# Attention weights: four of ten key tiles turned by DMA in 16-bit halves instead of by TensorE, with the value product placed later

## Chip, cores and metric

The kernel runs on one core of one Trainium2 chip. The metric is the device time of one execution in microseconds (us), lower is better. Engines are TensorE (PE in the rows; PEld its weight loads), VectorE (DVE), ScalarE (ACT), GpSimd (POOL) and SyncE (SP), which here only issues DMAs.

## What is computed

One step of a hybrid backbone over 1024 latent tokens and 128 prompt tokens: a modulated norm, an input projection, a gated MLP, a pooling mixer and latent attention side by side, an output projection, then 16 expert-choice routed experts. The change is in the attention alone. All is float32.

```python
def attention(q, k, v):
    ...
    def block(qi):
        s = jnp.einsum('bqhd,bkhd->bhqk', qi, k).astype(jnp.float32) * ATTN_SCALE
        pr = jax.nn.softmax(s, axis=-1).astype(v.dtype)
        return jnp.einsum('bhqk,bkhd->bqhd', pr, v)
```

There are 8 heads with 64 value columns each. A latent query sees 1280 keys (1024 latent, 256 cached); a prompt query sees the 128 prompt keys.

## The kernel before

The attention runs from about 274 to 650 us. It works on head pairs: four groups i = 0 to 3 of two heads. A group has 18 score tiles n = 0 to 17; tile n is token tile t = n // 2 and head j = n % 2. Tiles 0 to 15 are 128 latent queries by 1280 keys (ten key tiles of 128), tiles 16 and 17 are the prompt's, 128 by 128.

For one tile n the steps are:

- `score` (line 881, TensorE): 128 queries by 512, 512 and 256 keys into three PSUM banks. Two sets of three banks alternate, so score n waits for the exponential of n-2.
- `highest` (lines 1863 and 1865, VectorE): the row maximum over 1280 columns, and its negation.
- `exponential` (line 1455, ScalarE): exp into the SBUF tile `prob[n % 2]`, with row sums.
- `scaled` (lines 1884 and 1886, VectorE): reciprocal of the sum, and the weights times it, in place. It raises `norm_ok`.
- `turn` (line 915, TensorE): ten 128x128 transposes in three chunks (4, 4 and 2 key tiles) into PSUM banks 6 and 7.
- `turned` (line 1443 ScalarE, line 1897 VectorE): each chunk copied to `probT`. VectorE takes the first chunk of odd tiles, ScalarE all others.
- `weigh` (line 930, TensorE): for two tiles at once (both heads of a token tile), ten key tiles of values times `probT`, in one PSUM bank; `weighed` (line 1877, VectorE) copies it out.

Every engine runs its instructions in the order in which they are written. `attend` of each engine is a loop over n = 2, 4, ..., 14 and a written-out last part. TensorE's last part also takes `fill(0)` to `fill(5)`: the next group's query and key projections, or in the last group four half tiles of the output projection. `MID_ORDER` lists who takes banks 6 and 7 in turn. After a group, `scores_values` makes the next group's values and first two score tiles.

SyncE's queue loads in the attention the next group's weights (`head_queries`, `head_keys`) and moves the rope rows of the next group's queries (`move_queries`, line 535). In the last group it loads the 4 MB of output weights and, before the attention, two tiles of the input rows (`x_again`). GpSimd has nothing to do from before the attention to its last part, where it adds `x_again` to the output rows (line 2461).

The expert stage, later, already turns two arrays by DMA in 16-bit halves: 128 rows of 1024 float32 are split into high and low 16-bit halves by VectorE, turned by `dma_start_transpose` (512 KB; lines 606 and 615) and joined by VectorE (lines 2273 and 2281).

## Time and profile before

| | |
|---|---|
| median of 3 runs | 1561.43 us (1561.3 to 1561.96) |
| the profiled execution | 1561.85 us |
| its span | 1560.0 us |
| TensorE granted clock, mean | 0.996 |
| TensorE, VectorE, ScalarE, GpSimd busy | 98%, 39%, 27%, 7% |
| attention, four groups | about 274 to 650 us |
| experts | from 781 us on |

The span runs from the first to the last instruction of the profiled execution. Busy time is the time in which an engine has at least one instruction in it. Matmuls are pipelined: a matmul's record is longer than its distance to the next, so the pace of TensorE is read from the distance of starts.

### The profile page before, as it was taken

The numbers are of one execution on the slowest core, as the hardware profiler recorded it, in microseconds if no ns is written. First come the engines' busy times: TensorE is split into PE (matmuls) and PEld (weight loads), VectorE is DVE, ScalarE is ACT, GpSimd is POOL, SyncE is SP. The second block draws the span as 40 slices with busy tenths as digits, with TensorE's granted clock in tenths as the row PEclk, the third lists the DMA queues.
The fourth block names the chain that finished last, engine by engine and source line by source line (L and its number), as shares of the span: only waits on it lengthen the run. The fifth ranks groups of instructions, "written<-read, shape, count | busy, mean of one in ns | idle before, by whom it ended". The sixth has DMA issues, their size and how long they took to land.

```text
span 1560.0 us, 25914 instructions
## 1 busy us (share of the span) xinstructions
PE 1529.3 (98%) x10585; PEld 1224.9 (79%) x10585; DVE 607.6 (39%) x1389; ACT 423.0 (27%) x965; POOL 106.8 (7%) x108
## 2 busy tenths in 40 slices
PE   6999999999999999999999999999999999999997
PEld 3654545666666676544599999999999999999996
DVE  2211546675657576125666222222222222222215
ACT  2400112555545454223522111111111111111114
POOL 0005300000000000111000001000000000000000
PEclk9999999999999999999999999999999999999998
DMA  9970002001010300262278899999899899899885
GB/s 366 349 251 35 31 2 65 8 1 27 0 27 0 120 9 1 69 215 95 102 282 307 284 297 360 304 302 297 316 301 360 297 299 303 308 309 354 282 267 223
DMA packets 178634, 305.21 MB, mean 196 GB/s; under 512 B 73811, under 2 KB 75386, under 8 KB 176398
## 3 DMA queue, kind: packets, MB, share of 16 engines
q1 hardware_dynamic: 173534, 286.01, 52.5%
q0 software_dynamic: 4752, 17.30, 4.3%
q8 instruction: 43, 0.70, 0.2%
q10 hardware_dynamic: 288, 1.05, 0.2%
q14 instruction: 17, 0.14, 0.0%
HBM read 266.18 MB, written 21.64 MB: 184 GB/s over the span
## 4 chain that ended last, share of the span: by engine, by line
PE 93%; DVE 3%; DMA 1%; ACT 1%; issue 1%; SPq 0%; DVEq 0%; ACTq 0%; POOLq 0%
PE ps L1252 31%; PE ps L1281 16%; PE ps L881 9%; PE ps L644 8%; PE ps L982 7%; PE ps L930 5%; PE ps L915 4%; PE ps L669 2%; PE ps L835 2%; PE ps L659 1%; PE ps L847 1%; PE ps L860 1%; PE ps L676 1%; DMA wreg<-x_rows 1%; PE ps L736 1%
## 5 line engine op out<-in xcount | busy, mean ns | idle before, releaser
L1252 PE MATMUL ps<-mreg,wreg 128*128 128x144 f32 x4096 | 506.3, 286 | 0.0
L1252 PEld LDWEIGHTS ps<-mreg,wreg 128*128 128x128 f32 x4096 | 503.4, 190 | 0.7 <-ACT hreg L1567 0.4
L1281 PE MATMUL ps<-mreg,wreg 128*128 128x144 f32 x2048 | 257.4, 287 | 1.9 <-DVE mreg L2299 1.9
L1281 PEld LDWEIGHTS ps<-mreg,wreg 128*128 128x128 f32 x2048 | 254.1, 191 | 2.3 <-DVE mreg L2299 2.2
L2299 DVE TENSOR_TENSOR mreg<-ps,mreg 128x144 f32<-128x144 f32 x128 | 39.4, 308 | 357.5 <-PE ps L1252 346.7
L881 PE MATMUL ps<-wreg 128*128 128x512 f32 (+2 forms) x400 | 171.7, 519 | 0.2
L1604 ACT ACTIVATE mreg<-ps 128x144 f32<-128x144 f32 x128 | 37.2, 291 | 426.1 <-PE ps L1252 426.1
L982 PE MATMUL ps<-wreg,mreg 128*128 128x512 f32 x288 | 130.8, 598 | 0.0
L644 PE MATMUL ps<-hreg,wreg 128*128 128x512 f32 (+1 forms) x400 | 128.9, 480 | 0.0
L915 PEld LDWEIGHTS ps<-const,hreg 128*128 128x128 f32 x648 | 79.8, 140 | 58.8 <-issue 39.3
L1863 DVE TENSOR_REDUCE stat<-ps 128x1 f32<-128x1280 f32 (+1 forms) x72 | 97.7, 1357 | 57.4 <-PE ps L881 57.3
L644 PEld LDWEIGHTS ps<-hreg,wreg 128*128 128x128 f32 x400 | 64.6, 191 | 62.2 <-issue 61.9
L1443 ACT ACTIVATE hreg<-ps 128x512 f32<-128x512 f32 (+2 forms) x172 | 82.1, 502 | 101.9 <-PE ps L915 100.2
L1455 ACT ACTIVATE hreg<-ps,stat 128x1280 f32<-128x1280 f32 (+1 forms) x72 | 88.1, 1223 | 69.0 <-DVE stat L1865 69.0
L1623 ACT ACTIVATE mreg<-ps,modT 128x128 f32<-128x128 f32 x128 | 47.0, 367 | 210.7 <-PE ps L1281 210.7
L2244 DVE COPY hreg<-mreg 128x256 uint16<-128x256 uint16 x112 | 33.1, 295 | 178.9 <-ACT hreg L1625 178.9
L915 PE MATMUL ps<-const,hreg 128*128 128x128 f32 x648 | 97.5, 274 | 0.0
L982 PEld LDWEIGHTS ps<-wreg,mreg 128*128 128x128 f32 x288 | 52.0, 190 | 54.1 <-issue 54.1
L930 PEld LDWEIGHTS ps<-hreg,wreg 128*64 128x64 f32 x1296 | 70.0, 137 | 22.6 <-ACT hreg L1443 15.3
L930 PE MATMUL ps<-hreg,wreg 128*64 128x128 f32 x1296 | 78.5, 275 | 0.9 <-ACT hreg L1443 0.9
L881 PEld LDWEIGHTS ps<-wreg 128*128 128x128 f32 x400 | 62.1, 190 | 15.5 <-issue 13.6
L1886 DVE TENSOR_SCALAR hreg<-hreg,stat 128x1280 f32<-128x1280 f32 (+1 forms) x72 | 60.1, 835 | 2.6
(305 smaller groups left out, 1123.1 us busy)
## 6 DMA issues: line engine op xcount, KB each, us to landing
wreg<-in_w_e_dram SPq DMA_DIRECT2D x96, 2048.0 KB, 11.9
wreg<-in_w_ada_dram SPq DMA_DIRECT2D x16, 1024.0 KB, 8.5
wreg<-in_w_ada_dram SPq DMA_DIRECT2D x16, 512.0 KB, 11.0
wreg<-in_x_sample_dram SPq DMA_DIRECT2D x8, 512.0 KB, 4.6
wreg<-in_w_out_dram SPq DMA_DIRECT2D x1, 4096.0 KB, 12.9
x_rows<-wreg SPq DMA_DIRECT2D x8, 512.0 KB, 2.8
xn_rows<-wreg SPq DMA_DIRECT2D x8, 512.0 KB, 2.8
wreg<-x_rows SPq DMA_DIRECT2D x8, 512.0 KB, 8.8
```

The lines of the kernel that those rows point to most:

```text
L644: mm = pe.matmul(bank[BANK[n]][:, 0:gn], w_in_sb[:, k, w_at + m * P:w_at + (m + 1) * P], hT[:, k, g0:g0 + gn], start=(k == 0), stop=(k == ...
L881: mm = pe.matmul(bank[3 * (n % 2) + ch][:, 0:kn], qT[:, j, t * P:(t + 1) * P], kT[:, j, k0:k0 + kn], start=True, stop=True)
L915: mm = pe.transpose(bank[MID_BANK[("turn", n, ch)]][:, a * P:(a + 1) * P], prob[n % 2][:, kt * P:(kt + 1) * P], ident)
L930: mm = pe.matmul(pv_at(t)[64 * j:64 * j + 64, :], v_sb[:, kt, 64 * j:64 * j + 64], probT[:, 2 * (t % 2) + j, src * P:(src + 1) * P], start ...
L982: mm = pe.matmul(bank[o_bank(x)], mixT[:, k, t * P:(t + 1) * P], w_out_sb[:, k, hf * 512:(hf + 1) * 512], start=(k == 0), stop=(k == KD - 1))
L1252: mm = pe.matmul(o[:, 0:CAP], w[s][:, k, (f % 4) * P:(f % 4 + 1) * P], xsT[b][:, k, :], start=(k == 0), stop=(k == KD - 1))
L1281: mm = pe.matmul(bank[4 + dm % 2][:, 0:CAP], w2[f // 4][:, f % 4, dm * P:(dm + 1) * P], hidT[:, f, :], start=(f == 0), stop=(f == 7))
L1443: act.activation(probT[:, 2 * (t % 2) + j, ch * 512:ch * 512 + w], bank[MID_BANK[("turn", n, ch)]][:, 0:w], ACT.Copy).then_inc(t_out, 1)
L1455: act.activation(prob[n % 2][:, 0:w], src, ACT.Exp, bias=a_neg[:, n % 4:n % 4 + 1], scale=SCALE, accum_out=a_sum[:, n % 4:n % 4 + 1]).then ...
L1623: act.activation(yT[:, dm, :], bank[4 + dm % 2][:, 0:CAPS], ACT.Copy, scale=modT[:, 0, 40 + dm:41 + dm])
L1863: dve.tensor_reduce(a_max[:, r:r + 1], src, AX_X, ALU.max).then_inc(max_ok, 1)
L1886: dve.tensor_scalar(prob[n % 2][:, 0:w], prob[n % 2][:, 0:w], a_rec[:, r:r + 1], None, ALU.mult).then_inc(norm_ok, 1)
```

## The change

For score tiles 0 to 15 the first chunk (key tiles 0 to 3, 512 of 1280 columns) is no longer turned by TensorE. Instead:

- GpSimd (`split_prob`) copies the 512 float32 columns of `prob[n % 2]`, read as 1024 16-bit numbers, to `prob_halves[n % 2]`: first all low halves, then all high halves. It waits for `norm_ok` of n and for the transpose of n-2.
- SyncE (`turn_prob`) issues one DMA transpose of these 128 rows by 1024 halves (256 KB) to `prob_halves_T[n % 4]`.
- `joined(n)` writes the halves back in pairs to `probT`: ScalarE for even n, VectorE for odd n.
- `exponential(n)` also waits for the split of n-2, which reads the buffer that it overwrites.
- `weigh` takes key tiles 4 to 9 first, then 0 to 3 behind a wait for both joins. In the loop it stands behind all three score chunks of tile n instead of the first.
- The orders of the loops on TensorE, VectorE and ScalarE change. The maximum and the exponential of tile n-1 move to the iteration of n.
- In SyncE's queue the 16 transposes of a group stand ahead of `move_queries`. In the last group the output weights come in eight pieces, one behind each of the first eight transposes, and `x_again` is loaded behind the last joins.
- Waits on `t_mm` count 34 turns in a group instead of 50; the expert stage's waits on the shared semaphores start from the attention's count.

The core of the diff:

```diff
+        prob_halves = [view(wreg, 23232 + s * 512, 512).bitcast(U16) for s in range(2)]
+        prob_halves_T = [view(wreg, 16384 + s * 512, 512).bitcast(U16).rearrange("p (c q) -> p c q", q=P) for s in range(4)]
...
+        def join_prob(eng, copy, i, n):
+
+            t, j = divmod(n, 2)
+            eng.wait_ge((x_turned, y_turned)[j], (i * 8 + t + 1) * 16)
+            return copy(probT[:, 2 * (t % 2) + j, 0:512].bitcast(U16).rearrange("p (c h) -> p h c", h=2),
+                        prob_halves_T[n % 4].rearrange("p (h k) q -> p h (k q)", h=2))
...
-            for t in range(2):
-                sp.dma_start(x_again[t], tok_rows(x_sample, x_prompt, t)).then_inc(xa_in[t], 16)
...
-            for i in range(1, 4):
-                sp.wait_ge(wq_ok, i)
-                head_queries(i)
-                sp.wait_ge(proj_mm, i * 9)
-                head_keys(i)
-                sp.wait_ge(s_mm, i * 18)
-                move_queries(i)
+            def turn_prob(i, n):
+                sp.wait_ge(halves_split, prob_split(i, n))
+                sp.dma_start_transpose(out=prob_halves_T[n % 4], in_=prob_halves[n % 2]).then_inc((x_turned, y_turned)[n % 2], 16)
+            for i in range(3):
+                sp.wait_ge(wq_ok, i + 1)
+                head_queries(i + 1)
+                turn_prob(i, 0)
+                sp.wait_ge(proj_mm, (i + 1) * 9)
+                head_keys(i + 1)
+                for n in range(1, 16):
+                    turn_prob(i, n)
+                sp.wait_ge(s_mm, (i + 1) * 18)
+                move_queries(i + 1)
             sp.wait_ge(q_moved, 4 * 64)
-            sp.dma_start(w_out_sb, w_out[0].rearrange("(k p) f -> p k f", p=P)).then_inc(w_out_in, 16)
-            sp.wait_ge(proj_mm, 36)
-            sp.dma_start(flip_sb, flip_count).then_inc(flip_in, 16)
+            for n in range(16):
+                turn_prob(3, n)
+                if n < KD:
+                    sp.dma_start(w_out_sb[:, n, :], w_out[0, n * P:(n + 1) * P, :]).then_inc(w_out_in, 16)
+                if n == 1:
+                    sp.wait_ge(proj_mm, 36)
+                    sp.dma_start(flip_sb, flip_count).then_inc(flip_in, 16)
+            for t in range(2):
+                turn_out(sp, 3, 12 + 2 * t, 0)
+                turn_out(sp, 3, 13 + 2 * t, 0)
+                sp.dma_start(x_again[t], tok_rows(x_sample, x_prompt, t)).then_inc(xa_in[t], 16)
...
                 def weigh(t):
 
-                    if t < 7:
-                        turn_out(pe, i, 2 * t + 1, 0)
                     turn_out(pe, i, 2 * t + 1, 1 if t < NT - 1 else 0)
                     bank_free(("weigh", t))
-                    for kt in range(10) if t < NT - 1 else range(10, 11):
+                    for kt in (4, 5, 6, 7, 8, 9, 0, 1, 2, 3) if t < NT - 1 else (10,):
                         if kt == 8:
                             turn_out(pe, i, 2 * t + 1, 2)
+                        if kt == 0:
+
+                            turn_out(pe, i, 2 * t, 0)
+                            turn_out(pe, i, 2 * t + 1, 0)
                         for j in range(2):
                             src = kt if t < NT - 1 else 0
                             mm = pe.matmul(pv_at(t)[64 * j:64 * j + 64, :], v_sb[:, kt, 64 * j:64 * j + 64],
                                            probT[:, 2 * (t % 2) + j, src * P:(src + 1) * P],
-                                           start=(kt in (0, 10)), stop=(kt in (9, 10)))
+                                           start=(kt in (4, 10)), stop=(kt in (3, 10)))
                     mm.then_inc(pv_mm, 1)
 
                 for n in range(2, 16, 2):
                     score(i, n, 0)
+                    turn(n - 2, 1)
+                    score(i, n, 1)
+                    turn(n - 2, 2)
+                    score(i, n, 2)
                     if n >= 4:
                         weigh((n - 4) // 2)
-                    score(i, n, 1)
-                    turn(n - 2, 0)
-                    score(i, n, 2)
-                    turn(n - 2, 1)
-                    turn(n - 2, 2)
-                    for ch in range(3):
-                        score(i, n + 1, ch)
-                        turn(n - 1, ch)
+                    score(i, n + 1, 0)
+                    turn(n - 1, 1)
+                    score(i, n + 1, 1)
+                    turn(n - 1, 2)
+                    score(i, n + 1, 2)
...
+                def joined(n):
+
+                    join_prob(act, lambda out, src: act.activation(out, src, ACT.Copy), i, n).then_inc(t_out, 1)
+
                 def exponential(n):
 
                     act.wait_ge(neg_ok, i * 18 + n + 1)
                     if n >= 2:
 
-                        act.wait_ge(t_mm, i * 50 + 3 * (n - 1))
+                        if n < 16:
+                            act.wait_ge(t_mm, i * 34 + 2 * (n - 1))
+                        act.wait_ge(halves_split, prob_split(i, n - 2))
...
+                for n in range(2, 16, 2):
+                    if n >= 4:
+                        joined(n - 4)
+                    turned(n - 2, 1)
+                    if n >= 4:
+                        exponential(n - 1)
+                    turned(n - 2, 2)
                     exponential(n)
-                    if n >= 2:
-                        turned(n - 1, 1)
-                        turned(n - 1, 2)
-                    exponential(n + 1)
-                    turned(n, 0)
-                    if n < 16:
-                        turned(n, 1)
+                    turned(n - 1, 1)
+                    turned(n - 1, 2)
...
+                def joined(n):
+
+                    join_prob(dve, dve.tensor_copy, i, n).then_inc(t_out_d, 1)
+
                 scaled(0)
                 highest(i, 1)
                 values_out(i, 2)
                 scaled(1)
-                def turned(n):
-
-                    t, j = divmod(n, 2)
-                    dve.wait_ge(t_mm, i * 50 + turns_before(n, 0) + 1)
-                    dve.tensor_copy(probT[:, 2 * (t % 2) + j, 0:512], bank[MID_BANK[("turn", n, 0)]]).then_inc(t_out_d, 1)
-
                 for n in range(2, 16, 2):
+                    if n >= 4:
+                        highest(i, n - 1)
+                        joined(n - 3)
                     highest(i, n)
-                    turned(n - 1)
-                    highest(i, n + 1)
+                    if n >= 4:
+                        scaled(n - 1)
+                        weighed((n - 4) // 2)
                     scaled(n)
-                    weighed((n - 2) // 2)
-                    scaled(n + 1)
...
+            def split_prob(i, n):
+
+                pool.wait_ge(norm_ok, i * 18 + n + 1)
+                if n >= 2:
+                    pool.wait_ge((x_turned, y_turned)[n % 2], (i * 8 + n // 2) * 16)
+                pool.tensor_copy(prob_halves[n % 2].rearrange("p (h k) -> p h k", h=2),
+                                 prob[n % 2][:, 0:512].bitcast(U16).rearrange("p (k h) -> p h k", h=2)).then_inc(halves_split, 1)
+            for i in range(4):
+                for n in range(16):
+                    split_prob(i, n)
...
+DVE_JOINS = [(n, 0) for n in range(1, 16, 2)]
```

TensorE's loop, some iterations in. Line 881 (905 after) is score, 915 (939) turn, 930 (956) weigh; the rows without a tile are waits; `hreg` holds `prob` and `probT`, `wreg` the queries, keys and values. TensorE's loop before, from the wait ahead of an iteration's first score:

```order
L876 REGISTER_ALU
L881 MATMUL ps<-wreg 128x512
L428 REGISTER_ALU
L930 MATMUL ps<-hreg,wreg 64x128 x16
L428 REGISTER_ALU
L930 MATMUL ps<-hreg,wreg 64x128 x4
L881 MATMUL ps<-wreg 128x512
L915 MATMUL ps<-const,hreg 128x128 x4
L881 MATMUL ps<-wreg 128x256
L906 REGISTER_ALU
L915 MATMUL ps<-const,hreg 128x128 x4
L428 REGISTER_ALU
```

TensorE's loop after, from the last score chunk of tile n-1 to the first part of the value product:

```order
L905 MATMUL ps<-wreg 128x256
L900 REGISTER_ALU
L905 MATMUL ps<-wreg 128x512
L434 REGISTER_ALU
L939 MATMUL ps<-const,hreg 128x128 x4
L905 MATMUL ps<-wreg 128x512
L434 REGISTER_ALU
L939 MATMUL ps<-const,hreg 128x128 x2
L905 MATMUL ps<-wreg 128x256
L434 REGISTER_ALU
L956 MATMUL ps<-hreg,wreg 64x128 x12
L434 REGISTER_ALU
```

Before, an iteration starts with one score chunk, the value product, a chunk of scores, and then turns in three chunks of a tile. Now all three score chunks of a tile have the turns of chunks 1 and 2 between them, and the value product follows the third; its second part waits for the joins.

VectorE's loop. Line 1863 (1903 after) is the maximum, 1865 (1905) its negation, 1884 and 1886 (1924 and 1926) reciprocal and scaling, 1897 the eviction of a turned chunk, 1877 (1917) the copy of a value product, 440 the join (`wreg` holds `prob_halves_T`). VectorE's loop before, from the first maximum of an iteration:

```order
L1863 TENSOR_REDUCE stat<-ps 128x1 [waits s_mm]
L1865 TENSOR_SCALAR stat<-stat 128x1 [waits max_ok]
L1896 REGISTER_ALU
L1897 COPY hreg<-ps 128x512 [waits t_mm]
L1862 REGISTER_ALU
L1863 TENSOR_REDUCE stat<-ps 128x1 [waits s_mm]
L1865 TENSOR_SCALAR stat<-stat 128x1 [waits max_ok]
L1884 RECIPROCAL stat<-stat 128x1 [waits exp_ok]
L1886 TENSOR_SCALAR hreg<-hreg,stat 128x1280 [waits rec_ok]
L1876 REGISTER_ALU
L1877 ISA [waits pv_mm]
L1877 COPY mreg<-ps 128x128
```

VectorE's loop after, from the first maximum of an iteration:

```order
L1903 TENSOR_REDUCE stat<-ps 128x1 [waits s_mm]
L1905 TENSOR_SCALAR stat<-stat 128x1 [waits max_ok]
L439 ISA
L440 COPY hreg<-wreg 128x2x512 [waits y_turned]
L1902 REGISTER_ALU
L1903 TENSOR_REDUCE stat<-ps 128x1 [waits s_mm]
L1905 TENSOR_SCALAR stat<-stat 128x1 [waits max_ok]
L1924 RECIPROCAL stat<-stat 128x1 [waits exp_ok]
L1926 TENSOR_SCALAR hreg<-hreg,stat 128x1280 [waits rec_ok]
L1916 REGISTER_ALU
L1917 ISA [waits pv_mm]
L1917 COPY mreg<-ps 128x128
```

Before, VectorE evicts a chunk that TensorE turned between the two maxima. Now at this place it joins a chunk that a DMA turned, and the second maximum and the scaling behind it stand behind that DMA.

## Rows read from the trace of the kernel before

**Rows 1.** Page, part 1, and busy time of one whole group of the attention loop.

```profile
PE 1529.3 (98%) x10585; PEld 1224.9 (79%) x10585; DVE 607.6 (39%) x1389; ACT 423.0 (27%) x965; POOL 106.8 (7%) x108
364.00:454.00 90.00, 89.82 (x663) 61.91 (x662) 56.70 (x100) 48.93 (x88) 0.00 (x0) 1.00 0.05 12
```

**Rows 2.** Timeline, TensorE: start us, duration us, line, operation; one round.

```profile
389.28 2.40 PE L930 MATMUL ps<-hreg,wreg 128*64 128x128 f32 x40
...
391.61 1.12 PE L881 MATMUL ps<-wreg 128*128 128x512 f32 x2
...
395.00 0.60 PE L915 MATMUL ps<-const,hreg 128*128 128x128 f32 x4
...
395.43 1.02 PE L881 MATMUL ps<-wreg 128*128 128x512 f32 x2
...
398.34 2.40 PE L930 MATMUL ps<-hreg,wreg 128*64 128x128 f32 x40
```

**Rows 3.** Page, part 5: all 648 transposes; count, busy us, mean ns.

```profile
L915 PE MATMUL ps<-const,hreg 128*128 128x128 f32 x648 | 97.5, 274 | 0.0
```

**Rows 4.** Timeline, VectorE, of the same pair.

```profile
393.64 1.49 DVE L1863 TENSOR_REDUCE stat<-ps 128x1 f32<-128x1280 f32 x1 [0.32 <-PE ps L881]
...
395.63 0.69 DVE L1897 COPY hreg<-ps 128x512 f32<-128x512 f32 x1 [0.31 <-PE ps L915]
...
397.37 1.49 DVE L1863 TENSOR_REDUCE stat<-ps 128x1 f32<-128x1280 f32 x1 [1.04 <-PE ps L881]
...
398.96 0.15 DVE L1884 RECIPROCAL stat<-stat 128x1 f32<-128x1 f32 x1
...
399.15 0.89 DVE L1886 TENSOR_SCALAR hreg<-hreg,stat 128x1280 f32<-128x1280 f32 x1
```

**Rows 5.** Groups by line: 16-bit joins of the expert stage, and one ScalarE pass.

```profile
L2273 DVE COPY hreg<-hreg 128x2048 uint16<-128x2048 uint16 x14 | 18.4, 1318 | 0.0
L1502 ACT ACTIVATE wreg<-wreg 128x1024 f32<-128x1024 f32 x7 | 7.4, 1057 | 24.9 <-POOL wreg L2461 24.9
```

**Rows 6.** GpSimd's groups: instruction, count, busy us, mean ns.

```profile
L2461 POOL TENSOR_TENSOR wreg<-wreg 128x1024 f32<-128x1024 f32 x7 | 16.5, 2353 | 480.4 <-DVE wreg L1950 480.4
L2481 POOL COPY mreg<-hreg 128x128 f32<-128x128 f32 x16 | 12.7, 797 | 10.5 <-ACT hreg L1567 10.5
L2441 POOL MEMSET wreg<- 128x1184 f32 x2 | 2.2, 1084 | 14.9 <-DVE wreg L1769 14.9
```

**Rows 7.** Timeline: VectorE's scaling beside a GpSimd instruction, and without one.

```profile
630.68 0.69 DVE L1950 TENSOR_TENSOR wreg<-ps,g_rows 128x512 f32<-128x512 f32 x1 [6.39 <-PE ps L982]
...
631.45 2.35 POOL L2461 TENSOR_TENSOR wreg<-wreg 128x1024 f32<-128x1024 f32 x1 [390.34 <-DVE wreg L1950]
...
632.51 1.38 DVE L1886 TENSOR_SCALAR hreg<-hreg,stat 128x128 f32<-128x128 f32 x1
...
640.09 0.29 DVE L1886 TENSOR_SCALAR hreg<-hreg,stat 128x128 f32<-128x128 f32 x1
```

**Rows 8.** DMA issues: KB each, us from issue to landing.

```profile
wreg<-wreg SPq DMA_DIRECT2D x16, 144.0 KB, 2.5
hreg<-hreg SPq DMA_TRANSPOSE x14, 4.3
mreg<-mreg SPq DMA_TRANSPOSE x13, 16.2
```

**Rows 9.** One transpose of 512 KB: its issue on SyncE, then the DMA engines.

```profile
931.38 1.98 SPq L606 DMA_TRANSPOSE hreg<-hreg  x1
...
932.00:932.50 0.50, 0.50 (x6) 0.50 (x6) 0.00 (x0) 0.01 (x1) 0.00 (x0) 1.00 0.00 0
932.50:935.00 2.50, 2.50 (x22) 2.50 (x22) 0.64 (x2) 0.28 (x1) 0.00 (x0) 1.00 1.09 204
```

**Rows 10.** Timeline: the rope rows' move, and the next group's first scores.

```profile
440.24 2.42 SPq L535 DMA_DIRECT2D wreg<-wreg  x4
...
452.98 2.31 PE L881 MATMUL ps<-wreg 128*128 128x512 f32 x6
```

More of the change, by code:

```diff
@@ L382, in build, with prob_split @@
         x_turned, y_turned = sem("x_turned"), sem("y_turned")
+        def prob_split(i, n):
+            return i * 16 + n + 1
         def y_steps(e):
@@ L908, in turn @@
                 def turn(n, ch):
-                    if ch == 0:
+                    if ch < 2:
                         pe.wait_ge(norm_ok, i * 18 + n + 1)
@@ L2537, in turns_before @@
 def turns_before(n, ch):
[L2539 to L2547 removed]
+    return 2 * n + ch - 1 if n < 16 else 16 + n
+PROB_TURNS = 4 * 16
+DVE_JOINS = [(n, 0) for n in range(1, 16, 2)]
+ACT_TURNS = [u for n in range(2, 16, 2) for u in [(n - 4, 0)][:n // 4] + [(n - 2, 1), (n - 2, 2), (n - 1, 1), (n - 1, 2)]]
+ACT_TURNS += [(12, 0), (14, 0), (14, 1), (14, 2), (15, 1), (15, 2), (16, 0), (17, 0)]
+MID_ORDER = [u for n in range(2, 16, 2)
+             for u in [("turn", n - 2, 1), ("turn", n - 2, 2)] + [("weigh", (n - 4) // 2)][:n // 4]
+             + [("turn", n - 1, 1), ("turn", n - 1, 2)]]
+MID_ORDER += [("weigh", 6)] + [("turn", n, ch) for n in (14, 15) for ch in (1, 2)]
 MID_ORDER += [("turn", 16, 0), ("turn", 17, 0), ("weigh", 7), ("weigh", 8)]
```

62 lines of the change are left out of this document (33 added, 29 removed).

## The prediction

> **What bounds the kernel now.** I read the busy shares first, then one whole group of the attention loop, then one round of its inner loop in the timeline. TensorE has a matmul in flight for 98% of the span and for 89.8 of 90 us in the group at 364 to 454 us, at the full granted clock; VectorE works 56.7 us there, ScalarE 48.9 us, GpSimd not at all, and the DMA engines are 5% busy [rows 1]. A busy TensorE need not be at its peak, so I check the pace. One round (two 128-query score tiles of the same tokens, n and n+1) takes 398.34 - 389.28 = 9.06 us [rows 2]. In it four transposes go through in 395.43 - 395.00 = 0.43 us, 0.107 us each, with the next score right behind them; 0.107 and not the 274 ns of the record [rows 3] is what a transpose costs a full TensorE, since the record contains the pipeline. Twenty transposes are 2.14 us of the round, a value product (weigh) is near 2.3 us with its switch, and the rest is scores. So the attention loop is bound by TensorE's stream, and a transpose taken out is worth its 0.107 us, provided that nothing else comes to set the round.
>
> **What the change removes.** Four of ten transposes for each n below 16: 8 x 0.107 = 0.86 us of a round, which leaves 9.06 - 0.86 = 8.20 us. A group has 7 rounds in the loop (n = 2 to 14) and 8 more transposes in its last part. There are 4 groups. If TensorE stays the bound, the gain is 4 x (7 x 0.86 + 0.86) = 27.5 us. The five evictions of the first chunk's turned keys go as well: on VectorE 0.69 us [rows 4], on ScalarE one more.
>
> **What it adds, engine by engine.** For each n a GpSimd copy that splits 512 float32 weights into 1,024 16-bit halves, a DMA transpose of 256 KB on SyncE's queue, and a copy that joins the halves again, on VectorE for odd n and on ScalarE for even n.
>
> The join on VectorE: the same kind of copy over 2,048 halves takes 1.318 us [rows 5]. With about 0.15 us that doesn't depend on the size (my estimate, from the smallest VectorE instructions [rows 4]) half the size is 0.15 + 0.58 = 0.73 us, against 0.69 us for the eviction that it replaces. ScalarE's join, over 1,024 elements from SBUF, is taken as 1.06 us [rows 5]. ScalarE then works about 5.8 us of a round and VectorE about 6.4 us: by their sums neither is a bound.
>
> The split: no row shows it. Above it stands the GpSimd instruction that reads two streams of 1,024 elements and writes one, 2.35 us; below it the memset that only writes, 1.084 us for 1,184 elements, so 0.94 us for 1,024 [rows 6]. It reads one stream and writes one, so I take a value between, 1.5 us, and keep both ends. GpSimd then works some 3 us of a round. Farther off stands the copy of 128 elements in short pieces, 0.797 us, which is 6.2 ns an element [rows 6]; that is a rival below. The Trainium skill (GPSIMD Engine Reference, section on elementwise work) gives about 1.8 cycles an element for a tight loop, 512 elements in 769 ns; by it the split would be an estimated 1.54 us, and the sum would move by 0.04 us a round. The same page advises against GpSimd for elementwise work; here that matters only as far as the rounds below show.
>
> The DMA transpose: no row shows 256 KB. The expert stage has 512 KB: 4.3 us from issue to landing [rows 8]. Its data starts some 1.1 us after the issue, and runs at 204 GB/s for 2.5 us [rows 9], so 0.7 us come behind it. Half the data is 1.1 + 1.25 + 0.7 = 3.1 us. The bounds: 2.5 us, which a plain move of 144 KB takes, and 4.3 us [rows 8]. The other transpose's 16.2 us [rows 8] is time behind 4 MB of weights in the same queue; in the attention loop the DMA engines are nearly idle [rows 1], except in the last group, where eight 512 KB pieces of the output weights go between the transposes. I cost these at nothing: they come about once in 4 us and are read first in the tail. The Trainium skill (Advanced Engine Details and Errata, section on the X-bar transpose) expects 350 to 400 GB/s from a transpose. The trace differs, 204 GB/s, and the trace decides; by the page the transfer would be an estimated 0.6 us shorter, and TensorE would stay the bound.
>
> **The waits that it adds: the DMA round.** VectorE's new order in iteration n is: maximum n-1, join n-3, maximum n, scaling n-1, value out, scaling n. Behind join n-3 stand maximum n and scaling n-1, and scaling n-1 is what the split, the transpose and the join n-1 of the next iteration start from. So there is a closed round, once for two tiles: join 0.73; maximum, its negation, reciprocal and scaling in a row, 399.15 + 0.89 - 397.37 = 2.67 us [rows 4]; split 1.5; transfer 3.1; and five handoffs, of which the trace shows one (VectorE to GpSimd, 631.45 - 631.37 = 0.08 us [rows 7]), together some 0.3 us as an estimate. Sum: 0.73 + 2.67 + 0.3 + 1.5 + 3.1 = **8.3 us**. That is 0.1 us above TensorE's 8.20 us, and 0.76 us below 9.06. The round beats the old one as long as split plus transfer stay below 9.06 - 3.70 = 5.36 us; I have 4.6.
>
> The even tiles' joins on ScalarE come one iteration after the scaling plus a whole round, so they have some 4 us more, and the value product, which now takes keys 4 to 9 first and keys 0 to 3 last, has its joins ready. An exponential n now also waits for split n-2, since it overwrites the weights; that split ends over 3 us ahead of it.
>
> **The waits that it adds: the shared port.** A scaling of 128 elements takes 0.29 us alone, but 1.38 us where it starts while GpSimd's addition runs, and it ends at 633.89, right behind the addition's end at 633.80 [rows 7]. So a scaling that comes while a split runs waits for the split's end. The Trainium skill states the same (SBUF — State Buffer, Who interferes with whom: an exclusive lock for whole instructions); the trace agrees, with 1.38 against 0.29 us. Scaling n comes some 0.5 us behind scaling n-1, so split n-1 is in its way each time. This makes a second round: join, maximum, scaling n-1 (0.73 + 2.67), split n-1, scaling n (0.89), split n, and the join again if it also has to wait: 4.29 + 2 x (split + 0.17) = 7.6 us at a split of 1.5 us. It is below 8.2, so it costs nothing; at a split of 2.35 us it is 9.33 us, and it passes 9.06 at 2.2 us. The small weight scalings (0.3 us) come ahead of the split's handoff and cost nothing.
>
> **What is moved.** SyncE's queue now holds the transposes ahead of the rope rows' move for the next group. Before, that move is issued at 440.24 and the group's first score starts at 452.98 [rows 10]: 12.7 us for an issue of 2.4 us and a landing of 2.5 us [rows 8, 10]. It can come some 4 us later, behind transpose 15, and stays hidden. The value product of tile 7 and the prompt's stand behind the last fills, which gives joins 14 and 15 over 5 us. The reload of the input rows now stands behind these joins in the last group; each has two output products of 7 us of time. All these are put at nothing.
>
> **The sum.** 28 rounds x 0.76 = 21.3 us, and 32 transposes outside of them x 0.107 = 3.4 us: 24.7 us. The profiled execution took 1561.85 us and its span is 1560.0; the runs' median is 1561.43, 0.4 us lower. 1561.4 - 24.7 = **1537 us** (rounded).
>
> **Rivals.**
> 1. TensorE stays the bound (split plus transfer under 4.5 us): 27.5 us less, 1534. It differs from the forecast by 3 us and is counted with it. If the new order also loses switches of TensorE (0.5 us of a round is not stream), up to 4 us more: 1530.
> 2. The DMA round in between: split plus transfer at 4.9 to 5.2 us, round 8.6 to 8.9: 28 x 0.16 to 0.46 + 3.4 = 8 to 16 us less, 1545 to 1553. For it: both terms are interpolated, and both could be short by 0.3 us.
> 3. **Slower: the split is as slow as the two-stream addition.** At 2.35 us the port round is 9.33 us and the DMA round 3.70 + 2.35 + 3.1 = 9.15. TensorE then waits in every round: 28 x 0.27 - 3.4 = 4 us more, 1566. With the full transpose's 4.3 us as well, 10.35 us: 28 x 1.29 - 3.4 = 33 us more, 1594. It decides from a split of 2.2 us, or a sum of 5.36 us. For it: the nearest GpSimd row of the same length is just this one. Against it: half the reads.
> 4. The split costs by the element what the piecewise copy costs, 6.2 ns: 6.4 us, the port round 4.63 + 12.8 = 17.4 us, 28 x 8.4 = 235 us more, about 1793. Against it: that copy has 8 pieces of 16 elements, the split 2 of 512.
> 5. The gain isn't there because transposes weren't what TensorE was short of, within 3 us of 1561. The pace in rows 2 speaks against it.
>
> **Chances.** Forecast with rival 1: 0.55. Rival 2: 0.15. Rival 3: 0.22. Rival 4: 0.03. Rival 5: 0.05. For eight in ten I leave out rival 4, the far part of rival 3 and little below: 1530 to 1570. 0.2% is 3 us, about what a measurement of this kernel can tell from no change: faster 0.70, same 0.06, slower 0.24.
>
> **What would show it.** The round in the steady part of a group: 8.2 to 8.3 us, and TensorE's idle below 0.2 us a round. The split's mean near 1.5 us, the transpose's landing near 3.1 us. VectorE's join waiting for a DMA by a few tenths; that wait well over 1 us means rival 2 or 3. Scaling's mean rising from 0.89 us by some 0.4 us, half of them blocked. The forecast is wrong if split plus transfer exceed 5.36 us, if a join runs at half the rate that I took, or if the granted clock leaves 1.0 in the group because TensorE waits.

## The result, and the profile after

| | before | after |
|---|---|---|
| median | 1561.7 us (1561.3 to 1562.34, 4 runs) | 1535.84 us (1535.2 to 1536.37, 4 runs) |
| ratio | | 0.9835, 95% interval 0.9823 to 0.9848 |
| span of the profiled execution | 1560.0 us | 1533.9 us |

The changed kernel is 25.9 us faster; 1537 was forecast. The page's part 1 and the busy time of the same stretch of the attention loop, which answer to [rows 1]:

```profile
PE 1499.8 (98%) x10329; PEld 1196.6 (78%) x10329; DVE 614.5 (40%) x1393; ACT 439.1 (29%) x961; POOL 173.8 (11%) x172
364.00:454.00 90.00, 89.42 (x631) 59.38 (x630) 63.44 (x110) 54.64 (x89) 18.10 (x18) 1.00 0.32 63
```

TensorE runs 256 transposes fewer (4 key tiles x 16 x 4 groups) and is as full as before; VectorE, ScalarE and GpSimd work more; in this stretch the DMA engines go from 5% to 32% busy. TensorE's timeline shows the round, from one value product to the next (start, duration, line):

```profile
385.31 2.40 PE L956 MATMUL ps<-hreg,wreg 128*64 128x128 f32 x40
393.46 2.40 PE L956 MATMUL ps<-hreg,wreg 128*64 128x128 f32 x40
```

The round is 393.46 - 385.31 = 8.15 us, for 9.06 in [rows 2]. The added work, in rows of three views: GpSimd's split and the two joins (groups by line: count, busy us, mean ns, idle before), and the transposes (DMA issues of the second group: us from issue to landing).

```profile
L2507 POOL COPY wreg<-hreg 128x1024 uint16<-128x1024 uint16 x64 | 66.4, 1038 | 291.4 <-DVE hreg L1926 288.2 <-DMA wreg<-wreg 3.2
L440 DVE COPY hreg<-wreg 128x1024 uint16<-128x1024 uint16 x32 | 23.9, 748 | 2.0 <-DMA wreg<-wreg 1.9
L1473 ACT ACTIVATE hreg<-wreg 128x1024 uint16<-128x1024 uint16 x32 | 43.2, 1350 | 0.0
wreg<-wreg SPq DMA_TRANSPOSE x16, 3.1
```

VectorE's join waited for a transpose only twice in 32 times, 1.9 us in all. Its timeline, which answers to [rows 4], says what it waits for instead (idle before in brackets):

```profile
384.25 0.75 DVE L440 COPY hreg<-wreg 128x1024 uint16<-128x1024 uint16 x1
385.42 1.49 DVE L1903 TENSOR_REDUCE stat<-ps 128x1 f32<-128x1280 f32 x1 [0.42 <-PE ps L905]
...
387.21 0.89 DVE L1926 TENSOR_SCALAR hreg<-hreg,stat 128x1280 f32<-128x1280 f32 x1
...
388.86 1.01 DVE L1926 TENSOR_SCALAR hreg<-hreg,stat 128x1280 f32<-128x1280 f32 x1
...
390.76 1.49 DVE L1903 TENSOR_REDUCE stat<-ps 128x1 f32<-128x1280 f32 x1 [0.69 <-PE ps L905]
```

Both maxima still wait for TensorE's scores, 0.42 and 0.69 us: TensorE is the bound. From a group's first value projection (line 860, 884 after) to the next group's it took 89.45, 89.46 and 89.45 us before, and 84.26, 82.76 and 82.76 after; the last group, up to the output product behind its last value product, took 104.23 and 97.89. That is 5.2, 6.7, 6.7 and 6.3 us less, 24.9 of the span's 26.1; the last 1.2 us lie behind the attention.

The first group gains 1.5 us less than the next two. The chain of waits (start, us, what) shows why: one of its last transposes landed after 4.75 us, and VectorE's join and all behind it stood in its line.

```profile
337.55 4.75 DMA wreg<-wreg
...
342.32 0.06 DVE hreg L440
```

This is one execution. The stretch that holds it, between the value products of token tiles 6 and 7, took 13.94 us here and 12.44 in the second group; in the profile of the kernel with its keys in order, below, it took 12.43 in the first group too.

### The profile page after: what moved, and what is told of

It reads as the page before. It is cut to its first block, busy times and chain, and to the rows that moved or that the text cites. A ratio compares the mean times of both kernels' runs of the same rounds, so it can differ in the third digit from the quotient of the medians.

```text
span 1533.9 us, 25610 instructions
## 1 busy us (share of the span) xinstructions
PE 1499.8 (98%) x10329; PEld 1196.6 (78%) x10329; DVE 614.5 (40%) x1393; ACT 439.1 (29%) x961; POOL 173.8 (11%) x172
## 3 DMA queue, kind: packets, MB, share of 16 engines
q10 hardware_dynamic: 288, 1.05, 0.2%
## 4 chain that ended last, share of the span: by engine, by line
PE 89%; DVE 3%; DMA 3%; issue 3%; ACT 1%; POOL 1%; SPq 0%; DVEq 0%; ACTq 0%; POOLq 0%
PE ps L1277 32%; PE ps L1306 16%; PE ps L668 8%; PE ps L1007 8%; PE ps L905 6%; PE ps L956 4%; PE ps L693 2%; PE ps L939 2%; DMA wreg<-wreg 2%; PE ps L683 1%; PE ps L859 1%; PE ps L871 1%; PE ps L884 1%; PE ps L700 1%; DVE stat L1903 1%
## 5 line engine op out<-in xcount | busy, mean ns | idle before, releaser
L905 PE MATMUL ps<-wreg 128*128 128x512 f32 (+2 forms) x400 | 168.3, 520 | 2.0 <-ACT hreg L1486 2.0
L939 PEld LDWEIGHTS ps<-const,hreg 128*128 128x128 f32 x392 | 49.8, 141 | 68.1 <-issue 54.7
L2507 POOL COPY wreg<-hreg 128x1024 uint16<-128x1024 uint16 x64 | 66.4, 1038 | 291.4 <-DVE hreg L1926 288.2
L2546 POOL DMA_INDIRECT x_rows<-hreg,idx_s x15 | 23.9, 1596 | 531.4 <-DVE hreg L2321 519.9
L1468 ACT ACTIVATE hreg<-ps 128x512 f32<-128x512 f32 (+2 forms) x136 | 63.1, 476 | 67.9 <-PE ps L939 65.5
```

What stands on the lines that cost most here:

```text
L905: mm = pe.matmul(bank[3 * (n % 2) + ch][:, 0:kn], qT[:, j, t * P:(t + 1) * P], kT[:, j, k0:k0 + kn], start=True, stop=True)
L939: mm = pe.transpose(bank[MID_BANK[("turn", n, ch)]][:, a * P:(a + 1) * P], prob[n % 2][:, kt * P:(kt + 1) * P], ident)
L1468: act.activation(probT[:, 2 * (t % 2) + j, ch * 512:ch * 512 + w], bank[MID_BANK[("turn", n, ch)]][:, 0:w], ACT.Copy).then_inc(t_out, 1)
L2507: pool.tensor_copy(prob_halves[n % 2].rearrange("p (h k) -> p h k", h=2), prob[n % 2][:, 0:512].bitcast(U16).rearrange("p (k h) -> p h k", ...
```

## Experiments

All are edits of the changed kernel; ratios are to the kernel before, with their 95% intervals. The baseline is 1535.84 us.

### No join: what the added work costs

```diff
             for i in range(4):
                 for n in range(16):
-                    split_prob(i, n)
```
with `turn_prob` and both `joined` emptied likewise, and the waits on them gone.

> Leaves out all that the change adds: no split, no DMA transpose, no join; key tiles 0 to 3 of the weights are never turned, so the value product reads stale numbers there. TensorE's order is that of the changed kernel. Theory A (TensorE's stream sets the round of 8.15 us, and split, transpose and join are hidden): the round stays at 8.1 to 8.15 us, and only the 1.5 us that the end of the first group lost in the profile come back: 1533 to 1535.5 us. Rival B (one of the new rounds of waits sets the 8.15 us): the round falls to 8.0 us or less, 28 x 0.15 = 4 us or more, 1531 us or less.

Measured: 1534.95 us (1533.38 to 1536.1), ratio 0.983 [0.9817, 0.9844]. The round in its trace is 8.15 us as well (value products at 391.37 and 399.52). Split, transfer and both joins together cost 0.9 us, and the ranges of the two kernels overlap. The added work is hidden.

### Two chunks fewer: is TensorE still the bound?

```diff
                     score(i, n, 1)
-                    turn(n - 2, 2)
                     score(i, n, 2)
```
and the same for n - 1, with its evictions and waits.

> The changed kernel without the turns and evictions of key tiles 8 and 9 (they are left out, so the value product reads stale numbers there): TensorE's part of a round falls by 4 x 0.107 = 0.43 us, from 8.15 to 7.72 us, split, transpose and join stay. Theory A with the DMA round as the next bound (join 0.75 + 2.67 + handoffs 0.3 + split 1.04 + transfer 3.1 = 7.86 us): the round becomes 7.8 to 7.9 us, and VectorE's joins start to wait for the DMA: 28 x 0.3 + 1.7 = 10 us less, 1526 us. If TensorE still sets it, 7.72 us, 28 x 0.43 + 1.7 = 14 us less, 1522 us. If a new round already sets 8.15 us, no gain in the rounds: 1534 us.

Measured: 1524.43 us (1523.96 to 1524.99), ratio 0.9762 [0.9748, 0.9775]. The chain of waits from one value product to the next consists of TensorE alone; its second part:

```profile
398.73 1.72 PE ps L905 x5
400.45 0.44 PE ps L939 x4
400.89 1.29 PE ps L905 x4
402.18 2.33 PE ps L954 x40
```

The round fell to 7.71 us (394.40 to 402.11): 8.15 - 4 x 0.107 = 7.72. So at 7.71 us TensorE was still the bound, and the DMA round that I had put at 8.3 us must be shorter than that.

The time is 2.4 us above the 1522 that I expected for this case. Two rounds of the last group make it up, with 9.03 and 8.94 us (537.79 to 546.82 to 555.76). In the first, VectorE's join waited for a transpose:

```profile
539.01 0.74 DVE L440 COPY hreg<-wreg 128x1024 uint16<-128x1024 uint16 x1 [2.02 <-DMA wreg<-wreg]
```

The two transposes issued there among the pieces of the output weights (534.06 and 535.97) landed after 4.9 and 5.1 us, for 3.1 at the median. In the second, VectorE prepares the routing tables (2.5 us, from 544.00) ahead of a maximum.

### The transpose and the split, each done twice

The first issues each transpose once more, into spare rows and ahead of the real one; the second makes each split twice, the first time into a spare place. Each also waits until its spare place is free.

```diff
+                sp.dma_start_transpose(out=spare..., in_=prob_halves[n % 2]).then_inc(spare_in, 16)
                 sp.dma_start_transpose(out=prob_halves_T[n % 4], ...)
```
```diff
+                pool.tensor_copy(spare..., prob[n % 2][:, 0:512]...).then_inc(pool_step, 1)
                 pool.tensor_copy(prob_halves[n % 2]..., prob[n % 2][:, 0:512]...).then_inc(halves_split, 1)
```

> Ahead of each DMA transpose a second one of the same 256 KB into an unused place, so the one that counts lands some 1.25 us later (256 KB at 204 GB/s), at about 4.35 us. GpSimd, VectorE and their port are as before. Theory (DMA round): 0.75 + 2.67 + 0.3 + 1.04 + 4.35 = 9.1 us, 28 x 0.95 = 27 us more, 1563 us, with VectorE's join waiting for the DMA. Rival (the transfer is hidden with more than a microsecond to spare, since only 8.15 us of TensorE count): 1536 us.

> GpSimd makes the split twice, the first time into an unused place, and signals after the second: split 2.07 us and, with its second wait, perhaps 2.2. DMA round 3.72 + 2.1 + 3.1 = 8.9 us, port round 4.31 + 2 x 2.27 = 8.85 us: 28 x 0.75 = 21 us more, 1557 us. This is the prediction's threshold rule (split plus transfer over 5.36 us gives back the gain): the sum is 5.2 us here, so the round should come out 0.15 us below the 9.06 us of the kernel before. Rival (the two rounds add their waits): 9.5 us and over, 1575 us.

Measured: 1558.78 us (1557.24 to 1561.2), ratio 0.9985 [0.9975, 0.9994], with the transpose twice; 1559.23 us (1558.05 to 1561.1), 0.9986 [0.9976, 0.9995], with the split twice. Rounds: 8.93 us (408.31 to 417.24) and 9.13 us (408.74 to 417.87). Each has taken back nearly the whole gain. The chain of waits of the split done twice is the closed round (handoffs of 0.02 us left out):

```profile
400.40 0.06 DVE hreg L441
400.45 0.59 issue
401.04 1.49 DVE stat L1904
...
402.56 0.15 DVE stat L1906
402.71 0.08 DVE stat L1925
...
402.82 0.90 DVE hreg L1927
403.71 0.05 issue
403.76 1.04 POOL hreg L2511
404.80 1.58 POOL wreg L2513
...
406.40 3.10 DMA wreg<-wreg
```

From landing to landing (400.38 to 409.51): join 0.66, maximum to scaling 2.67, handoff 0.05, the extra split 1.04, the real one 1.58, transfer 3.10 and 0.03: 9.13 us. The real split takes 1.58 and not 1.04 us because VectorE's scaling of tile n gets in between the two; so the round is longer than the 8.9 us expected. Without the extra split, and with the other at its 1.04 us alone, the changed kernel's DMA round is 9.13 - 1.04 - 0.54 = 7.55 us. That is 0.6 us below TensorE's 8.15. The transpose done twice agrees: its extra issue is 1.23 us of the chain and the transfer 0.11 longer, and 8.93 - 1.23 - 0.11 is 7.59. It came 4 us below the 1563 expected, with a round of 8.93 for 9.1.

### A second GpSimd copy: the port round

```diff
+                pool.tensor_copy(spare..., g1_rows[:, 0, 0:512]...).then_inc(pool_step, 1)
```
behind each split; it reads rows that nothing waits for and writes to a place that nobody uses.

> Behind each split, after its signal, GpSimd makes a second copy of the same form between two places that nobody else uses at the time. The transfer isn't delayed; only the port is held longer, 2.07 us instead of 1.04. Theory (port round): 4.31 + 2 x (2.07 + 0.17) = 8.8 us, 28 x 0.64 = 18 us more, 1554 us, with scalings of over 1.3 us and joins of over 0.75 us. Rival (VectorE's scaling and join don't wait for a 16-bit copy of GpSimd, the 1.38 us of before was the two-stream addition's): 1536 us.

Measured: 1537.43 us (1537.16 to 1538.15), ratio 0.9843 [0.9827, 0.9859]. My expectation missed by 17 us. The timelines of VectorE and of GpSimd show what happened:

```profile
387.07 0.89 DVE L1927 TENSOR_SCALAR hreg<-hreg,stat 128x1280 f32<-128x1280 f32 x1
...
388.73 1.01 DVE L1927 TENSOR_SCALAR hreg<-hreg,stat 128x1280 f32<-128x1280 f32 x1
389.66 1.05 DVE L1709 TENSOR_SCALAR hreg<-xreg,vT 128x128 f32<-128x128 f32 x1
390.64 1.48 DVE L1904 TENSOR_REDUCE stat<-ps 128x1 f32<-128x1280 f32 x1
...
393.44 1.49 DVE L1904 TENSOR_REDUCE stat<-ps 128x1 f32<-128x1280 f32 x1 [0.23 <-PE ps L906]
```
```profile
388.02 1.04 POOL L2508 COPY wreg<-hreg 128x1024 uint16<-128x1024 uint16 x1 [3.35 <-DVE hreg L1927]
389.01 1.63 POOL L2513 COPY hreg<-g_rows 128x1024 uint16<-128x1024 uint16 x1
```

The split runs from 388.02 to 389.06; scaling n, there since 388.73, gets through at 1.01 us, only 0.12 longer than alone. The extra copy starts at 389.01 and is the one that is held: 1.63 us, for 1.03 in most of the others. In its turn it holds the next small VectorE scaling, 1.05 us for 0.28. The two engines take turns; a second GpSimd instruction does not extend the first one's hold. VectorE's waits for TensorE's scores shrank from 0.69 and 0.42 us to none and 0.23; the round stayed at 8.15 us (393.33 to 401.48). So the sum behind my port round, in which a scaling waits for the whole of what GpSimd has queued, is wrong. What a single much longer split would do wasn't tried.

### The order of keys in the value product

```diff
-                    for kt in (4, 5, 6, 7, 8, 9, 0, 1, 2, 3) if t < NT - 1 else (10,):
+                    for kt in range(10) if t < NT - 1 else (10,):
```

> The value product takes key tiles 0 to 9 in order again, so it waits for both joins before its first product. In the profile of the changed kernel VectorE's join ends at 385.00 and the value product starts at 385.31, so by theory A nothing changes in a round: 1536 us within 1 us. By the rival, that the order of the keys hides the transfer, each round loses some of the 1.3 us that six key tiles take, over 0.2 x 28 = 6 us: 1542 us or more.

Measured: 1536.02 us (1535.26 to 1536.51), ratio 0.9836 [0.9823, 0.985], round 8.15 us. In the changed kernel the join ends at 385.0 and the product starts at 385.31: the order of keys is worth nothing that shows.

### The value product's place

The change moved the product behind the three score chunks of the even tile. First I undid that on both engines: on TensorE it stands behind the first chunk again, on VectorE its copy-out stands ahead of the maximum of tile n.

```diff
                     score(i, n, 0)
+                    if n >= 4:
+                        weigh((n - 4) // 2)
                     turn(n - 2, 1)
                     score(i, n, 1)
                     turn(n - 2, 2)
                     score(i, n, 2)
-                    if n >= 4:
-                        weigh((n - 4) // 2)
```

> The value product stands behind the first score chunk of tile n again, as before the change, instead of behind the third, and VectorE copies it out ahead of the second maximum. The joins are then due 1.7 us earlier (TensorE waits some 0.4 us for them behind six key tiles), and the second maximum comes 2 us later, so its exponential ends some 0.3 us after the next round's first score could start. Theory: a round of 8.5 to 8.9 us, 10 to 21 us more, 1546 to 1557 us. Rival (TensorE's work is the same, so its place is free): 1536 us.

Measured: 1610.29 us (1609.05 to 1615.48), ratio 1.0319 [1.0299, 1.0339], 53 us above the top of what I expected. The round is 10.95 us (405.43 to 416.38). TensorE stands three times in it, for VectorE's join, for an exponential and for VectorE's scaling of tile n-1:

```profile
407.39 1.09 PE L956 MATMUL ps<-hreg,wreg 128*64 128x128 f32 x16 [0.42 <-DVE hreg L440]
...
411.07 1.12 PE L905 MATMUL ps<-wreg 128*128 128x512 f32 x2 [0.48 <-ACT hreg L1486]
...
413.42 0.65 PE L939 MATMUL ps<-const,hreg 128*128 128x128 f32 x4 [1.23 <-DVE hreg L1926]
```

I had reckoned with the first two, at 0.4 and 0.3 us, and not with the third and longest; the three are 2.1 of the 2.8 us. Next I moved the product by one place alone, TensorE's order only, and worked the round out ahead of the run.

```diff
-                    score(i, n, 2)
                     if n >= 4:
                         weigh((n - 4) // 2)
+                    score(i, n, 2)
```

> The changed kernel with the value product only one place earlier on TensorE, ahead of the last piece of scores of the even tile instead of behind it; VectorE's order stays. Theory (the maximum of the even tile now waits for join, value product and last scores in a row): from one maximum of an even tile to the next, 4.65 us of VectorE's steps up to the maximum of the odd tile (5.34 from 385.42 to 390.76, less the wait of 0.69), 2.5 for that maximum and the join, 2.34 for the value product, 0.5 for the last scores and 0.1 of handoffs, 10.1 us for 8.15, on 28 rounds: 1536 + 28 x 1.95 = 1590 us (1575 to 1600). Rival (TensorE has slack elsewhere that takes it up, and only the 0.3 us between the join's end and the product's start counts): 1536 to 1548 us.

Measured: 1592.38 us (1591.34 to 1593.86), ratio 1.0199 [1.0182, 1.0216], round 10.34 us (403.06 to 413.40). The time is the forecast's 1590 within 2.4 us, but the chain of waits is not the forecast's, which ran from the join to the product:

```profile
403.13 2.33 PE ps L956 x40
405.46 0.64 PE ps L905 x2
...
406.13 1.50 DVE stat L1903
...
407.65 0.15 DVE stat L1905
407.81 0.08 DVE stat L1924
...
407.91 0.90 DVE hreg L1926
...
408.93 0.65 PE ps L939 x4
...
413.47 2.33 PE ps L956 x40
```

Product 2.33, last scores 0.64, maximum to scaling with the handoffs 2.83, and then TensorE's own work from the turn of tile n-1, which needs that scaling, to the next product, 4.54: 10.34 us. TensorE stands 1.98 us for the scaling in each round. The join is not in this chain: the product takes its keys last, and of VectorE's 32 joins TensorE's products waited for one, 0.5 us.

So the value product in its new place is what fills TensorE's time while VectorE takes the maximum of tile n and scales tile n-1 (2.67 us). In the changed kernel the scaling ends at 388.10 and the turn that needs it starts at 388.61. If the product stands ahead of the last scores, the maximum starts later by the product's 2.33 us, and behind the scores TensorE has one score chunk left to do before that turn. The forecast also counted 28 rounds; the product stands in the loop from n = 4 on, in 24 of them: 24 x 2.19 = 53 of the 56.5 us measured. That its 28 x 1.95 came so near is in part luck. The moved product is worth over twice the change's gain.

### Six of ten key tiles of even tiles: a version that should be faster

ScalarE and the DMA round had time left, so even tiles turn six key tiles by DMA and four on TensorE (splits of 1,536 halves, joins likewise).

```diff
+TURNED = (768, 512)
-                                 prob[n % 2][:, 0:512].bitcast(U16)...
+                                 prob[n % 2][:, 0:TURNED[n % 2]].bitcast(U16)...
```

> A further step: for even tiles, whose joins have a round more of time, six key tiles (0 to 5) go through the halves and TensorE turns 6 to 9 in one chunk; odd tiles as before. Theory A: two transposes less in a round, 8.15 - 0.21 = 7.94 us, and four more groups' ends: 32 x 0.214 = 6.8 us less, 1529 us. ScalarE's join of 1536 halves takes 1.9 to 2.0 us instead of 1.34, and it works some 7.3 us of a round. Rival: ScalarE or the transfer for odd tiles, which now waits behind 384 KB in the queue, is late: 1536 us or more.

Measured: 1567.69 us (1565.09 to 1569.69), ratio 1.0036 [1.0022, 1.005]. Yet its attention did what it should: rounds of 7.93 us (396.73 to 404.66; 8.15 - 2 x 0.107 = 7.94), and the experts start at 748.5 us, for 755.2. The loss is all behind that: from the first to the last product of the expert stage's hidden layer 783.3 us, for 744.9. TensorE's timeline and the busy time around one start of the expert loop's body show it, and the fetch queue's packets in the stretch 748 to 1500 us, first of the changed kernel, then of this one:

```profile
994.73 0.75 PE L1278 MATMUL ps<-mreg,wreg 128*128 128x144 f32 x4 [2.69 <-issue]
998.07 33.89 PE L1278 MATMUL ps<-mreg,wreg 128*128 128x144 f32 x252 [2.60 <-issue]
```
```profile
992.00:995.00 3.00, 0.31 (x3) 0.28 (x3) 0.29 (x1) 0.53 (x2) 0.00 (x0) 1.00 0.28 55
995.00:998.00 3.00, 0.48 (x4) 0.26 (x3) 0.00 (x0) 0.00 (x0) 0.00 (x0) 0.82 1.28 143
998.00:1000.00 2.00, 1.93 (x8) 1.93 (x9) 0.00 (x0) 0.00 (x0) 0.00 (x0) 0.50 1.04 399
1000.00:1002.00 2.00, 2.00 (x10) 2.00 (x10) 0.00 (x0) 0.29 (x1) 0.00 (x0) 0.50 1.01 397
```
```profile
q8 instruction: 18, 0.29, 0.2%
```
```profile
q8 instruction: 61, 1.00, 0.6%
```

TensorE waits there for nothing that the profile shows, and the queue that fetches instructions moves 43 packets more. With the stalls the granted clock falls to 0.50, TensorE's lower level of 1.2 GHz, for some 4 us. This happens at five starts of the loop's body (994.73, 1096.59, 1197.17, 1298.98, 1400.97), 38.4 / 5 = 7.7 us each. The experts' code is the same in both kernels, but 80 instructions of TensorE's compiled program ahead of it are gone, so it lies elsewhere. Three kernels try that, all by repeats of TensorE's first wait, which only move code.

```diff
                 if kind == "vecs":
+                    for _ in range(160):
                         pe.wait_ge(vecs_in, 16 * 8)
```
(two such waits make one instruction; 352 in the changed kernel.) In the third they are spread over the long matmuls of the projections:
```diff
                 for k in range(KD):
+                    if k in (1, 3, 5) or (k == 6 and n % 5 == 0):
+                        for _ in range(2):
+                            pe.wait_ge(vecs_in, 16 * 8)
                     mm = pe.matmul(bank[BANK[n]][:, 0:gn], w_in_sb...
```

> The kernel with six of ten key tiles of even tiles turned by DMA (label e8_six_of_even), and 80 instructions more on TensorE, all of them repeats of its first wait, where TensorE idles 4.2 us anyway (9.84 to 14.34 us). They move nothing but the place of the code behind them: the expert loop (1569 instructions of TensorE's compiled program) starts at instruction 8457 again, as in the changed kernel, not at 8377. In e8_six_of_even the experts began 6.7 us sooner than in the changed kernel (748.5 for 755.2), but at each pass of the loop TensorE then stood twice for 1.9 to 2.7 us with nothing awaited, and the queue of instruction fetches moved 61 packets in the expert stage where the changed kernel has 18. Theory (where the loop's code lies decides whether it is fetched anew at each pass): no such gaps, 18 packets, and 1536 - 6.7 = 1529 us (1526 to 1532). Rival (the loss is the kernel's own, by its transfers or buffers): 1567 us as before.

> The changed kernel with 176 such instructions more on TensorE at its first wait, so that the expert loop starts at instruction 8633 and ends at 10202: counted in blocks of 256 instructions, 33.72 to 39.85 where the changed kernel has 33.04 to 39.16 and e8_six_of_even had 32.72 to 38.85. Nothing else is changed. Theory (the place of the loop's code decides): the loss of e8_six_of_even comes to the changed kernel too, 1567.7 - 1529 = some 38 us: 1574 us (1565 to 1582, the upper end with up to 8 us for the added waits themselves), with gaps at each pass of the loop and about 60 fetch packets in the stage. Rival (it has another cause): 1536 us, or up to 1540 with the waits.

> The kernel of e8_six_of_even once more, with 81 instructions more on TensorE, so that its expert loop starts at instruction 8458; but here they lie one by one between the long matmuls (128x512, 480 ns each) of the projections ahead of the attention, not in a row at the first wait. In e9_six_padded the 80 in a row cost 0.105 us each: TensorE's first matmul came at 18.25 us, not 9.84, and the experts began at 757.5, not 748.5; the loop itself had lost its gaps (18 fetch packets, nothing idle in it), and 1529 + 9 = 1538 is what was measured. Theory (the place of the loop's code decides, and an added instruction between long matmuls is issued while the one ahead of it runs): experts from 748.5 to 749.5, no gaps, 1528 to 1531 us. Rival (each added instruction holds TensorE up wherever it stands): 1529 + 81 x 0.105 = 1537.5 us. If the loop is fetched anew at each pass all the same: 1567 us or more.

| kernel | loop's code, instructions of TensorE's compiled program | fetch packets | idle in its first products | median |
|---|---|---|---|---|
| changed | 8457 to 10026 | 18 | 0.0 us | 1535.84 us |
| six of even | 8377 to 9946 | 61 | 23.6 us | 1567.69 us |
| six, padded in a row | 8457 to 10026 | 18 | 0.0 us | 1538.74 us (1538.18 to 1539.41) |
| changed, padded by 176 | 8633 to 10202 | 60 | 24.4 us | 1594.21 us (1592.83 to 1594.76) |
| six, padding spread | 8458 to 10027 | 18 | 0.0 us | 1530.68 us (1528.87 to 1532.75) |

Ratios of the last three: 0.9857 [0.9841, 0.9874], 1.0212 [1.0195, 1.023], 0.9803 [0.9789, 0.9816]. Moving the same loop brings the stalls and takes them away, in either kernel. The waits in a row had a price that I hadn't counted for the first of these kernels (9 us for 80, with TensorE's first matmul at 18.25 for 9.84) and had put too low in the second: there the experts start at 773.2, 18.0 us late for 176, and 1536 + 18 + 38 = 1592. Spread between long matmuls, 81 cost 1.4 us (experts at 749.9 for 748.5). The last kernel is 5.2 us faster than the changed one: both ranges lie apart.

Which positions are bad isn't settled. The loop also ran without stalls from instruction 8717 (before), 8433 (no join), 8469 (product early) and 8318 (two chunks fewer), and with them only from 8377 and 8633.

## Why the prediction was right, point by point

- **TensorE's stream bounds, and a transpose is worth 0.107 us**: right. The round fell by 0.91 us, of which 8 x 0.107 is 0.86; the other 0.05 may be the new order's, which wasn't run by itself. Two chunks fewer took another 0.44 for 0.43. (The "five evictions" of the prediction are two a round.)
- **The bound afterwards**: the forecast had the DMA round 0.1 us above TensorE's 8.20; the runs give 7.55 and 8.15. This step was wrong, and TensorE stays the bound. So rival 1, which I had counted with the forecast, is what happened. By it the attention should have gained 27.4 us (256 x 0.107) and gained 24.9: the first group lost 1.6, its late transpose, the last 0.5, the others 0.15 each. That the total came so near 1537 is in part chance: 1.2 us behind the attention made up for half of it. Where the last group's 0.5 and those 1.2 us come from wasn't followed; its longest round (8.54 us) has a like in the kernel before (9.42), in both with VectorE's routing tables in it.
- **The terms of the DMA round**: transfer 3.1, measured 3.10. Join 0.73, measured 0.748. Maximum to scaling 2.67, measured 2.67. The split was mis-sized: 1.5, measured 1.04, close to the lower bound of 0.94 from the memset, not to the middle. Beside the 1.8 cycles that I quoted, the Trainium skill (GPSIMD Engine Reference, 3.1 Elementwise) gives 1.03 cycles an element for bodies that only the ports bound. By it the split would be an estimated 1,024 x 1.03 / 1.2 GHz = 0.88 us and what starting it costs, for which the page has no figure on GpSimd; the trace has 1.038 in all. It agrees with this rate and not with the 1.8 cycles: the splits of 1,536 halves in the kernel with six of ten key tiles take 1.471 us, 0.43 more for 512 elements, or 0.85 ns an element, where 1.03 cycles are an estimated 0.86 and 1.8 cycles 1.5. Handoffs 0.3: about 0.1 in the chain, since the maximum starts 0.65 us after the join's start, before the join's record ends.
- **ScalarE's join**: taken as 1.06 us from a float32 pass of 1,024 elements, measured 1.35. Nothing hangs on it here: ScalarE's joins waited for no transpose, and no value product for them.
- **The threshold** of 5.36 us for split plus transfer: the rule holds, the figure was 0.3 us low. With the split twice the sum is 1.04 + 1.58 + 3.10 = 5.72 and the round 9.13, hardly over the old one; from that run the threshold is 9.06 - 3.41 = 5.65 us.
- **The port**: the scaling that meets a split goes from 0.89 to 1.01, and the mean of the 64 from 0.887 to 0.940, not by some 0.4. The split's record ends 0.33 us behind the scaling's start and cost it 0.12, about 0.2 us less than the overlap. The same gap stands in [rows 7]: 1.29 us of overlap, 1.09 of delay. Whether the port is let go early or the records are off isn't shown; the split was also shorter than reckoned. The port round's sum is refuted as a way to price more GpSimd work: each engine waits at most for what the other has begun. The Trainium skill (SBUF — State Buffer, Who interferes with whom) says as much, whoever starts first has the port for the whole instruction; the runs agree, with 1.05 for 0.28 us on VectorE and 1.63 for 1.03 on GpSimd. I had drawn a sum from it in which only VectorE ever waits.
- **Moves put at nothing**: rope rows, key order and reload cost nothing that shows. The output weights' pieces hold transposes up: those issued at 548.34, 556.50 and 565.44, right behind a piece, landed after 4.5 to 4.6 us. In the changed kernel VectorE's joins waited only 0.3 us for transposes in that whole group; with rounds of 7.71 us one join waited 2.02 us. So the pieces cost nothing only as long as there is slack. The value product's new place was argued from its joins alone; the two earlier places cost 57 and 74 us, and not for the joins: the product fills TensorE's time behind the scores of tile n, of which the prediction says nothing.
- **Rival 3**, the slow split, lost at the row that it rested on: the two-stream addition's 2.35 us says nothing of a one-stream copy of 16-bit halves at 1.04.

## What to carry to other kernels

Where two engines hold each other's inputs in fixed orders, write down every closed round through both and add up its terms, then check in the trace that the waits are the ones you added: the moved product's round was forecast at 10.1 us and came out at 10.34, by another chain. An engine's longest piece of work belongs where the engine would otherwise wait for the other's answer. Before a variant is given up, see in which stage it lost its time: the faster attention was hidden behind a loop that had moved by 80 instructions. When a price lies between two bounds, look which of them the operation is like, one stream or two, rather than take the middle.

## What the runs showed of the hardware

- The same loop of 1,569 TensorE instructions runs with 18 fetch packets in the expert stage from some places of the program, and from two others with 60 or 61, that is 8 or 9 more at each of five starts of its body, with 3.8 to 5.3 us of standing still and then about 4 us at the lower clock: 7.7 us a start.
- A GpSimd copy and a VectorE scaling exclude each other, and either can be the one that waits: a 128-element scaling 1.05 us for 0.28, a GpSimd copy 1.63 for 1.03.
- GpSimd splits 1,024 16-bit elements in 1.04 us and 1,536 in 1.47; ScalarE joins as many in 1.35 us, VectorE in 0.75.
- Transposes of 256 KB land after 3.1 us at the median. In the first three groups one took 4.75 us and cost its group 1.5; why it was late isn't shown. In the last group three issued right behind a 512 KB piece of weights took 4.5 to 4.6 us, and in the kernel with two chunks fewer 4.9 and 5.1.
- TensorE issues repeats of a met wait at 0.105 us an instruction; between matmuls of 480 ns they cost nearly nothing.
